# The recurrent core of an RWKV-7 block: one mask for the whole triangle, and a new order of work on four engines

## The chip, the cores and the metric
One core of a Trainium2 chip runs the kernel. The metric is the time on the device, in microseconds (us), of one execution. TensorE multiplies matrices, VectorE and ScalarE work element by element, GpSimd does small side jobs, and SyncE issues DMAs.

## What is computed
The reference runs two transformer blocks over 1024 tokens of width 1024. The part at hand is the third mixer of the first block, `rwkv7_time_mix`, with 6 heads of 64 columns:

```python
def step(state, inp):
    r_t, w_t, k_t, v_t, kk_t, a_t = inp
    sa = jnp.einsum('bhvk,bhk->bhv', state, kk_t)
    state = (state * w_t[:, :, None, :]
             - sa[..., :, None] * (kk_t * a_t)[..., None, :]
             + v_t[..., :, None] * k_t[..., None, :])
    return state, jnp.einsum('bhvk,bhk->bhv', state, r_t)
...
_, out = lax.scan(step, state0, tuple(seq_first))
```

A 64x64 state per head is scaled, corrected and added to at each of the 1024 tokens, and read out with `r`. Everything else of the two blocks (projections, the two other mixers, normalizations, two feed-forward networks, a second block with its own mixers) lies before and behind this part and is not changed.

## The kernel before
The kernel is written for each engine by itself. Every engine has its own program in a fixed order, and semaphores tie the programs together: `did(eng, ins, name)` (L280) raises a semaphore when an instruction ends and makes the engine wait for it, and `wait_ge` holds an engine for another one. There is no planner. An engine that waits holds everything written behind the wait.

The core (L429 to L692) replaces the scan by chunks of `CH` = 128 tokens, `NC` = 8 of them. Three **units** i = 0, 1, 2 hold two heads h each, and each half q of a chunk has 64 tokens, so that most products are 64x64. All are in float32, which is why the trace has two records for each product and only one for a transpose. Per chunk, in TensorE's order (`core_pe`, L585):
- **Transposes** (L594) of Z, B, KK and VV into `bank_a(i)`. ScalarE copies them to `seqmaj` (L509).
- **Score products** (L600): B and KK against Z and R, four products of 64x256 a unit, filling both PSUM banks of the unit. VectorE copies the 128x1024 result under a causal mask by `copy_predicated` with `keep` (`scores_copy`, L548).
- **Triangle products** (L611): Z against B within and across the halves. `first_inverse` (L552) puts them into the unit matrix that GpSimd has laid down (L500).
- **Values** (L620): scores times VV for the three units, into `PT[3]`; ScalarE copies them (L511).
- **Levels** (L625): five steps for blocks 2, 4, 8, 16, 32 invert the unit triangular matrix. In each, x = triangle times inverse (4 products a unit), then VectorE multiplies x by the level's mask from `const` (`x_masked`, L567), then t = inverse times masked x (8 products a unit, 4 in the last level), then VectorE adds t to the inverse (L572, L575).
- **Solves** (L645 to L663): three steps of 64x128 products with a copy by ScalarE after each (L515, L518, L521).
- **R and G** (L664), with an addition and a copy by VectorE (L578, L579); **outputs** o (L671) and **states** g (L676) of which most is multiplied before it is known how the chunk's state enters; then the two products with the scaled state (L682). ScalarE copies the output (L524), and VectorE makes the next state (L582). At the head of each chunk VectorE scales the state twice (L546, L547).

`bank_a(i)` and `bank_b(i)` are the two 512-column halves of the PSUM tensor `PT[i]`. SyncE's queue and the DMAs play no part in the core beyond loads for later stages, issued before it (L695). Ahead of the core stand the projections up to `o2` (L590 waits for it), behind it the group norm of the core's output (`after_core_pe`, L740).

## Time and profile before

| what | value |
|---|---|
| median of 3 runs | 2602.79 us (2601.04 to 2603.61) |
| profiled execution, span | 2601.7 us |
| the core in it | 370.7 to 601 us |
| TensorE, VectorE, ScalarE, GpSimd busy in the span | 94%, 56%, 34%, 35% |
| granted clock of TensorE, mean | 0.971 of full speed |

The profiled execution's own time is this span; it lies 1.1 us under the median of the runs and among them. In the rows further down times count from the start of the span. PE is TensorE, PEld its loads of weights, DVE VectorE, ACT ScalarE, POOL GpSimd. A form such as `64*128 64x256` is the shape of the weights' tile in the array (rows\*columns), then that of the moving operand. A view that merges records names the form of the first. The granted clock is given as a share of 2.4 GHz, and has two levels, 1.0 and 0.5 (1.2 GHz).

### The profile page before, as it was taken

The page shows a single profiled execution, that of the slowest core. Times are in us where ns is not written, and L with a number is a line of the kernel's source. Part 1 is how long each engine was busy: PE and PEld are TensorE (multiplying, and loading weights), DVE is VectorE, ACT ScalarE, POOL GpSimd, SP SyncE. Part 2 cuts the span into 40 slices and gives each one's busy share as a digit, 9 for nine tenths or more (in the row PEclk, how much of TensorE's full clock was granted, in tenths as well). Part 3 has the DMA queues.
Part 4 walks back from the last instruction along what each step waited for, and adds up shares of the span by engine and source line. Part 5 has one row for each costly group of instructions (what it writes and reads, how often), then busy time and mean ns, then how long its engine had stood idle before and what let it go on. Part 6 is the DMA issues. An engine that isn't in the chain of part 4 may idle for free.

```text
span 2601.7 us, 36870 instructions
## 1 busy us (share of the span) xinstructions
PE 2453.7 (94%) x14984; PEld 1447.0 (56%) x15146; DVE 1453.3 (56%) x1727; ACT 887.3 (34%) x1105; POOL 907.3 (35%) x502
## 2 busy tenths in 40 slices
PE   4989999999889999999998999999889999999997
PEld 1645558886445555555554566675345555555553
DVE  5975666663487640466405794355587640466414
ACT  3255422221145431354313323321155431255314
POOL 0312110000236532455324798101236531455331
PEclk7999999999999999999998999989999999999999
DMA  8611030000302122211313613300121122211322
GB/s 330 236 47 49 14 110 3 3 3 17 121 9 65 50 89 107 88 53 62 120 34 137 112 52 94 124 1 25 41 89 49 65 88 99 97 49 65 118 72 84
DMA packets 55369, 199.91 MB, mean 77 GB/s; under 512 B 5792, under 2 KB 15520, under 8 KB 52256
## 3 DMA queue, kind: packets, MB, share of 16 engines
q1 hardware_dynamic: 47424, 179.98, 20.5%
q10 hardware_dynamic: 7776, 17.56, 1.9%
q8 instruction: 120, 1.97, 0.3%
q14 instruction: 49, 0.40, 0.1%
HBM read 168.16 MB, written 29.36 MB: 76 GB/s over the span
## 4 chain that ended last, share of the span: by engine, by line
PE 77%; DVE 11%; POOL 4%; issue 3%; DMA 3%; ACT 2%; SPq 0%; ACTq 0%; DVEq 0%; POOLq 0%; another core or an unknown queue 0%
PE pt L1163 16%; PE pt L1169 15%; PE pt L1166 15%; PE pt L1748 10%; PE pt L587 7%; PE pt L425 3%; PE pt L728 2%; PE pt L2625 2%; PE pt L2631 2%; PE pt L2628 2%; DMA work<-in_w_mod 1%; DVE work L550 1%; PE pt L346 1%; PE pt L411 1%; DVE work L2883 1%
## 5 line engine op out<-in xcount | busy, mean ns | idle before, releaser
L1113 POOL TENSOR_TENSOR slots<-work,weights_rounded 128x512 bf16<-128x512 f32 (+2 forms) x239 | 435.1, 1820 | 607.4 <-ACT weights_rounded L1285 317.6
L1166 PE MATMUL pt<-work,weights_rounded 128*128 128x512 bf16 x1208 | 327.5, 385 | 2.2
L1163 PE MATMUL pt<-rounded,weights_rounded 128*128 128x512 f32 x624 | 210.4, 454 | 11.4 <-POOL slots L1113 5.9
L587 PE MATMUL pt<-work 64*64 64x64 f32 (+5 forms) x4512 | 212.0, 244 | 6.7 <-DVE work L550 5.5
L1163 PE MATMUL pt<-rhs_rounded,weights_rounded 128*128 128x512 f32 x624 | 210.6, 454 | 7.2 <-DVE work L845 4.2
L587 PEld LDWEIGHTS pt<-work 64*64 64x64 f32 (+3 forms) x4512 | 192.8, 142 | 26.0 <-DVE work L550 7.7
L1163 PE MATMUL pt<-hidden_rounded,weights_rounded 128*128 128x512 f32 x704 | 203.5, 424 | 0.3
L1166 PEld LDWEIGHTS pt<-work,weights_rounded 128*128 128x128 bf16 x1248 | 100.1, 99 | 169.1 <-issue 98.2
L1169 PE MATMUL pt<-hidden_rounded,slots 128*128 128x512 bf16 x691 | 176.6, 387 | 1.1
L1169 PE MATMUL pt<-rhs_rounded,slots 128*128 128x512 bf16 x607 | 168.9, 391 | 1.4 <-issue 0.2
L1169 PE MATMUL pt<-rounded,slots 128*128 128x512 bf16 x607 | 168.7, 390 | 1.4 <-issue 0.2
L1279 ACT ACTIVATE weights_rounded<-work 128x512 fp32r<-128x512 f32 x196 | 123.8, 632 | 132.5 <-PE pt L1169 127.3
L1166 PE MATMUL pt<-slots,weights_rounded 128*128 128x512 bf16 x674 | 166.9, 381 | 1.3
L1163 PEld LDWEIGHTS pt<-hidden_rounded,weights_rounded 128*128 128x128 f32 x704 | 131.8, 188 | 41.6 <-POOL slots L1113 2.4
L1113 POOL TENSOR_TENSOR slots<-slots,weights_rounded 128x512 bf16<-128x512 f32 (+1 forms) x86 | 128.8, 1497 | 65.2 <-ACT weights_rounded L1279 62.6
L1285 ACT ACTIVATE weights_rounded<-work 128x1408 fp32r<-128x1408 f32 x37 | 51.1, 1382 | 293.0 <-PE pt L1169 292.7
L1662 POOL TENSOR_TENSOR slots<-slots,weights_rounded 128x1024 bf16<-128x1024 f32 x28 | 66.7, 2382 | 238.6 <-ACT weights_rounded L2058 237.5
L1163 PEld LDWEIGHTS pt<-rounded,weights_rounded 128*128 128x128 f32 x624 | 118.5, 190 | 54.6 <-issue 8.2
L1163 PEld LDWEIGHTS pt<-rhs_rounded,weights_rounded 128*128 128x128 f32 x624 | 118.5, 190 | 50.3 <-issue 5.4
L2599 POOL TENSOR_TENSOR slots<-slots,weights_rounded 128x1024 bf16<-128x1024 f32 x21 | 56.6, 2696 | 238.5 <-ACT weights_rounded L2754 238.2
L1432 DVE TENSOR_TENSOR slots<-pt,slots 128x512 f32<-128x512 f32 x120 | 83.0, 691 | 86.7 <-PE pt L1169 84.1
L1166 PEld LDWEIGHTS pt<-slots,weights_rounded 128*128 128x128 bf16 x704 | 63.9, 98 | 92.5 <-issue 31.0
(393 smaller groups left out, 4089.8 us busy)
## 6 DMA issues: line engine op xcount, KB each, us to landing
work<-in_w_up SPq DMA_DIRECT2D x64, 512.0 KB, 4.0
work<-in_w_down SPq DMA_DIRECT2D x37, 704.0 KB, 4.1
work<-in_w_mod SPq DMA_DIRECT2D x10, 2048.0 KB, 8.5
slots<-in_w_in SPq DMA_DIRECT2D x31, 512.0 KB, 3.6
slots<-in_w_up SPq DMA_DIRECT2D x24, 512.0 KB, 4.8
x_scratch<-work ACTq DMA_DIRECT2D x16, 512.0 KB, 2.7
work<-x_scratch SPq DMA_DIRECT2D x16, 512.0 KB, 8.6
slots<-in_w_v SPq DMA_DIRECT2D x10, 512.0 KB, 4.1
```

What stands on the lines that cost most here:

```text
L425: ins = pe.matmul(pt(name)[:, h * 512:h * 512 + 512], weights(k), w(s)[:, h * 512:h * 512 + 512], start=(k == 0), stop=(k == n - 1))
L587: return pe.matmul(out, lhs, rhs, start=start, stop=stop, skip_group_check=True)
L728: ins = pe.matmul(pt(f"o{m}")[:, h * 512:h * 512 + 512], w(WRAW + (NJOBS1 + m) % 2)[:, k * P:(k + 1) * P], w(s)[:, h * 512:h * 512 + 512], ...
L1113: did(pool, pool.tensor_tensor(dst, raw, high.bitcast(F32), ALU.subtract), name)
L1163: pe.matmul(out, whi[:, k * P:k * P + P], rhs_hi(k), start=first and k == ks[0], stop=False, skip_group_check=True)
L1166: pe.matmul(out, top_half(whi)[:, k * P:k * P + P], rhs_lo(k), start=False, stop=False, skip_group_check=True)
L1169: ins = pe.matmul(out, wlo[:, k * P:k * P + P], top_half(rhs_hi(k)), start=False, stop=last and k == ks[-1], skip_group_check=True)
L1279: did(act, act.activation(flat_hi(fast_block(half, j, p), 512), block_raw(half, j, BLOCKS[p]), ACT.Copy), "ffn_w_hi")
L1432: did(dve, dve.tensor_tensor(dst, src0, src1, ALU.add), "ffn_post")
L1662: G_(pool.tensor_tensor(p1_lo(n), p2_raw(n), p1_hi(n).bitcast(F32), ALU.subtract), "w_split")
L1748: return pe.matmul(o, l, r, start=start, stop=stop, skip_group_check=True)
L2599: did(pool, pool.tensor_tensor(p1_lo(n), p1_raw(n), p1_hi(n).bitcast(F32), ALU.subtract), "w_split")
```

## The change
- **Masks.** The level masks in `const` are turned over, and VectorE multiplies the raw triangle by all five at once when it is there (`begin`, 128x640 from PSUM into `CD[i]`). x then comes out masked, and ScalarE copies it to SBUF instead of VectorE multiplying it (`x_kept`).
- **Inverse in two places.** Even chunks keep it in `CB_[i]`, odd ones in `CD[i]`. So the next chunk's triangle products and `begin` are written between this chunk's level 4 and its solves.
- **Scores between levels.** The products of a unit become KK against Z and R (64x256), B against R (64x128) and only one 64x64 corner of B against Z, each head in a bank of its own; they and their copies (two of 128x448 a unit) stand between the levels. The transposes stand between levels 0 and 1.
- **States in the next chunk.** Outputs and state products of chunk c - 1 (`ends`) stand inside level 0 of chunk c, in `bank_b`, unit by unit; the new state is made by VectorE after the adds of level 0. The last chunk's state isn't made. GpSimd scales the states.

TensorE's matrix work is otherwise the same. The diff, cut: the lines removed are those of the functions printed above, and of those added `solves` (the old code with the new names), some declarations and blank lines are left out.

```diff
-put(f"level{b}", (r64 // (2 * b) == k64 // (2 * b)) & ((r64 // b) % 2 == 1) & ((k64 // b) % 2 == 0))
+put(f"level{b}", (r64 // (2 * b) == k64 // (2 * b)) & ((r64 // b) % 2 == 0) & ((k64 // b) % 2 == 1))
...
+def crossing(i, h):
+    return w(CA[i])[half(0), h * 512 + 64:h * 512 + 128]
...
+def level_t(i, h, n, rows):
+    at = 128 + h * 320 + n * 64
+    return w(CD[i])[rows, at:at + 64]
...
+def score_bank(i, h):
+    return (bank_b(0), bank_b(1), bank_b(2), bank(7), bank_b(0), bank_b(1))[2 * i + h]
...
+def inverse(c, i):
+    return w(CD[i])[:, 768:1024] if c % 2 else w(CB_[i])[:, 0:256]
...
+    def units(c):
+        for i in range(3):
+            if c > 1:
+                pool.wait_ge(E("solve_done"), 9 * (c - 2) + 6 + i + 1)
+            did(pool, pool.tensor_copy(inverse(c, i).rearrange("p (x n) -> p x n", x=4),
+                                       const("unit").unsqueeze(1).to_broadcast([P, 4, 64])), "inverse_unit")
+    units(0)
+    pool.wait_ge(E("p_end"), 3)
+    for c in range(NC):
+        if c < NC - 1:
+            units(c + 1)
+        for i in range(3):
+            if c > 0:
+                pool.wait_ge(E("state_new"), 3 * (c - 1) + i + 1)
+            did(pool, pool.tensor_scalar(s_scaled(i), state(i), small(PMID + 8 * i + c), None, ALU.mult), "pool_step")
+            did(pool, pool.tensor_scalar(s_ended(i), s_scaled(i), small(PEND + 8 * i + c), None, ALU.mult),
+                "state_scaled")
+def core_act(act):
+    act.wait_ge(E("core_zeroed"), 6)
+    def x_kept(c, n, i):
+        act.wait_ge(E("x_done"), 15 * c + 3 * n + i + 1)
+        did(act, act.activation(xbuf(i), x_of(i), ACT.Copy), "x_kept")
+    def o_kept(c):
+        for i in range(3):
+            act.wait_ge(E("o_done"), 3 * c + i + 1)
+            did(act, act.activation(w(Z + i)[:, c * CH:(c + 1) * CH], bank_b(i)[:, 256:384], ACT.Copy), "o_kept")
     for c in range(NC):
         for i in range(3):
+            x_kept(c, 0, i)
+        if c > 0:
+            o_kept(c - 1)
         for i in range(3):
             act.wait_ge(E("transposed"), 3 * c + i + 1)
-            did(act, act.activation(w(CC[i])[:, 0:512], bank_a(i), ACT.Copy), "seq_major")
+            did(act, act.activation(w(CC[i])[:, 0:512], bank_b(i), ACT.Copy), "seq_major")
+            x_kept(c, 1, i)
+        for n in range(2, 5):
+            for i in range(3):
+                x_kept(c, n, i)
...
+    o_kept(NC - 1)
...
+    def begin(c, i):
+        dve.wait_ge(E("inverse_unit"), 3 * c + i + 1)
+        dve.wait_ge(E("l_done"), c + 1)
+        V_(dve.copy_predicated(heads(inverse(c, i)), keep[:, 512:640].unsqueeze(1).to_broadcast([P, 2, P]), l_of(i)),
+           "inverse_ready")
+        V_(dve.tensor_tensor(w(CD[i])[:, P:768].rearrange("p (h b n) -> p h b n", h=2, b=5),
+                             l_of(i)[:, :, 64:P].unsqueeze(2).to_broadcast([P, 2, 5, 64]),
+                             level_masks(), ALU.mult), "levels_ready")
+    def add(c, n):
+        for i in range(3):
+            dve.wait_ge(E("t_done"), 15 * c + 3 * n + i + 1)
+            if n < 4:
+                V_(dve.tensor_tensor(inverse(c, i), inverse(c, i), t_of(i), ALU.add), "inverse_ready")
+            else:
+                turned = heads(inverse(c, i))[:, :, 64:P]
+                V_(dve.tensor_tensor(turned, turned, heads(t_of(i))[:, :, 64:P], ALU.add), "inverse_ready")
+    def scores_copy(c, i):
+        dve.wait_ge(E("products_done"), 3 * c + i + 1)
+        for h in range(2):
+            V_(dve.copy_predicated(w(CA[i])[:, h * 512 + 64:h * 512 + 512], keep[:, 64:512],
+                                   score_bank(i, h)[:, 64:512]), "scores_kept")
+    def state_next(c):
+        for i in range(3):
+            dve.wait_ge(E("o_kept"), 3 * c + i + 1)
+            dve.wait_ge(E("state_scaled"), 3 * c + i + 1)
+            V_(dve.scalar_tensor_tensor(state(i), bank_b(i)[:, 192:256], small(PEND + 8 * i + c), s_ended(i),
+                                        ALU.mult, ALU.add), "state_new")
+    for i in range(3):
...
+        add(c, 0)
+        if c > 0:
+            state_next(c - 1)
+        add(c, 1)
+        scores_copy(c, 0)
+        add(c, 2)
+        scores_copy(c, 1)
+        add(c, 3)
+        scores_copy(c, 2)
+        add(c, 4)
+        if c < NC - 1:
             for i in range(3):
+                begin(c + 1, i)
...
+    def l_products(c):
+        if c > 0:
+            pe.wait_ge(E("mv_kept"), c)
+        for i in range(3):
+            for x, (left, right) in enumerate(((Z + i, B + i), (B + i, Z + i))):
+                for h, q in ((0, 0), (1, 1), (0, 1), (1, 0)):
+                    at = h * 512 + i * P + x * 64
+                    ins = mm(PT[3][half(q), at:at + 64], w(left)[half(h), tok(c, q)], w(right)[half(h), tok(c, q)])
+        ins.then_inc(E("l_done"), 1)
+    def level_x(c, n):
+        for i in range(3):
+            pe.wait_ge(E("inverse_ready"), 18 * c + 3 * n + i + 1)
+            if n == 0:
+                pe.wait_ge(E("levels_ready"), 3 * c + i + 1)
+            for h in range(2):
+                for q in range(2):
+                    ins = mm(x_of(i)[half(q), h * 64:h * 64 + 64], level_t(i, h, n, half(q)),
+                             inv(c, i, h, 0, half(q)))
+            ins.then_inc(E("x_done"), 1)
+    def level_t_step(c, n):
+        for i in range(3):
+            pe.wait_ge(E("x_kept"), 15 * c + 3 * n + i + 1)
+            for h in range(2):
+                for q in range(2):
+                    if n < 4:
+                        mm(t_of(i)[half(q), h * P:h * P + 64], inv(c, i, h, 1, half(q)),
+                           xbuf(i)[half(q), h * 64:h * 64 + 64])
+                for q in range(2):
+                    ins = mm(t_of(i)[half(q), h * P + 64:h * P + P], xbuf(i)[half(q), h * 64:h * 64 + 64],
+                             inv(c, i, h, 1, half(q)))
+            ins.then_inc(E("t_done"), 1)
+    def transposes(c):
         for i in range(3):
             if c > 0:
                 pe.wait_ge(E("o_kept"), 3 * (c - 1) + i + 1)
+                pe.wait_ge(E("state_new"), 3 * (c - 1) + i + 1)
             for x, s in enumerate((Z + i, B + i, KK + i, VV + i)):
-                ins = pe.transpose(bank_a(i)[:, x * P:x * P + P], w(s)[:, tt], const("ident"))
+                ins = pe.transpose(bank_b(i)[:, x * P:x * P + P], w(s)[:, span_of(c)], const("ident"))
             ins.then_inc(E("transposed"), 1)
+    def products(c, i):
+        tt = span_of(c)
+        pe.wait_ge(E("seq_major"), 3 * c + (2, 3, 3)[i])
+        if i == 2:
+            pe.wait_ge(E("scores_kept"), 6 * c + 2)
+        for h in range(2):
+            mm(score_bank(i, h)[:, 256:512], w(KK + i)[half(h), tt], both(Z, i, 21, tt)[half(h)])
+        for h in range(2):
+            mm(score_bank(i, h)[:, 128:256], w(B + i)[half(h), tt], w(RR + i)[half(h), tt])
+        for h in range(2):
+            ins = mm(score_bank(i, h)[half(0), 64:128], w(B + i)[half(h), tok(c, 0)], w(Z + i)[half(h), tok(c, 1)])
+        ins.then_inc(E("products_done"), 1)
+    def values(c):
         for i in range(3):
+            pe.wait_ge(E("scores_kept"), 6 * c + 2 * i + 2)
...
+    def ends(c):
         for i in range(3):
             pe.wait_ge(E("r_ready"), 3 * c + i + 1)
+            pe.wait_ge(E("g_ready"), 3 * c + i + 1)
             pe.wait_ge(E("state_scaled"), 3 * c + i + 1)
             for h in range(2):
-                ins = mm(bank_a(i)[half(h), 256:384], s_scaled(i)[half(h)], rbuf(i)[half(h)], False, True)
+                mm(bank_b(i)[half(h), 256:384], zu(i)[:, h * P + 64:h * P + P], scores(i, h, 1), True, False)
+            for h in range(2):
+                mm(bank_b(i)[half(h), 256:384], seqmaj(i, 3, h), scores(i, h, 3), False, False)
+            for h in range(2):
+                ins = mm(bank_b(i)[half(h), 256:384], s_scaled(i)[half(h)], rbuf(i)[half(h)], False, True)
+            if c < NC - 1:
+                for h in range(2):
+                    mm(bank_b(i)[half(h), 192:256], seqmaj(i, 2, h), seqmaj(i, 3, h), False, False)
+                for h in range(2):
+                    mm(bank_b(i)[half(h), 192:256], seqmaj(i, 1, h), zu(i)[:, h * P + 64:h * P + P], False, False)
+                for h in range(2):
+                    ins = mm(bank_b(i)[half(h), 192:256], gbuf(i)[half(h)], s_scaled(i)[half(h)], False, True)
             ins.then_inc(E("o_done"), 1)
-            for h in range(2):
-                ins = mm(bank_b(i)[half(h), 192:256], gbuf(i)[half(h)], s_scaled(i)[half(h)], False, True)
-            ins.then_inc(E("chunk_done"), 1)
+    l_products(0)
+    for c in range(NC):
+        level_x(c, 0)
+        if c > 0:
+            ends(c - 1)
+        level_t_step(c, 0)
+        transposes(c)
+        level_x(c, 1)
+        level_t_step(c, 1)
+        products(c, 0)
+        level_x(c, 2)
+        products(c, 1)
+        level_t_step(c, 2)
+        level_x(c, 3)
+        products(c, 2)
+        level_t_step(c, 3)
+        level_x(c, 4)
+        values(c)
+        level_t_step(c, 4)
+        if c < NC - 1:
+            l_products(c + 1)
+        solves(c)
+    ends(NC - 1)
```

## Rows read from the trace of the kernel before

**Rows 1.** Page, busy time and share; the core's stretch by engine (busy PE, PEld, DVE, ACT, POOL; clock; DMA).
```profile
PE 2453.7 (94%) x14984; PEld 1447.0 (56%) x15146; DVE 1453.3 (56%) x1727; ACT 887.3 (34%) x1105; POOL 907.3 (35%) x502
...
370.70:601.00 230.30, 223.15 (x4608) 203.18 (x4608) 155.51 (x408) 52.22 (x128) 8.40 (x21) 0.98 0.04 13
```

**Rows 2.** Timeline, TensorE: first transpose of chunks 0, 3, 4, 5; first product behind the core.
```profile
370.73 1.53 PE L598 MATMUL pt<-cst,work 128*128 128x128 f32 x12 [1.43 <-DVE work L737]
...
456.84 0.33 PE L598 MATMUL pt<-cst,work 128*128 128x128 f32 x1
...
484.98 0.33 PE L598 MATMUL pt<-cst,work 128*128 128x128 f32 x1
...
514.59 0.33 PE L598 MATMUL pt<-cst,work 128*128 128x128 f32 x1
...
601.05 2.38 PE L411 MATMUL pt<-work,cst 128*128 128x512 f32 x5 [0.50 <-ACT work L524]
```

**Rows 3.** Chain of waits, chunk 7: from level 0 to level 1.
```profile
579.56 3.69 PE pt L587 x92
583.27 2.51 PE pt L587 x72
```

**Rows 4.** Timeline, chunk 7: start, length, engine, line, count, idle before.
```profile
575.05 2.64 DVE L550 COPY_PREDICATED work<-keep,pt 128x1024 f32<-128x1024 int32 x2 [0.50 <-PE pt L587]
577.75 1.59 PE L587 MATMUL pt<-work 64*64 64x64 f32 x24 [0.46 <-DVE work L550]
...
579.56 20.99 PE L587 MATMUL pt<-work 128*128 128x64 f32 x484 [0.22 <-DVE work L550]
...
583.25 0.94 DVE L567 TENSOR_TENSOR work<-pt,cst 128x128 f32<-128x128 f32 x3
583.26 2.38 PEld L587 LDWEIGHTS pt<-work 64*64 64x64 f32 x72 [0.16 <-DVE work L572]
584.39 1.35 DVE L572 TENSOR_TENSOR work<-work,pt 128x256 f32<-128x256 f32 x3 [0.20 <-PE pt L587]
```

**Rows 5.** Views of single lines: length in ns as min/median/max.
```profile
L509 ACT ACTIVATE work<-pt x24: 597/597/599, 371.5 to 574.4; 128x512 f32<-128x512 f32 x24
...
L524 ACT ACTIVATE work<-pt x24: 277/277/277, 398.6 to 600.5; 128x128 f32<-128x128 f32 x24
...
L500 POOL COPY work<-cst x24: 400/400/614, 339.6 to 568.3; 128x256 f32<-128x256 f32 x24
...
L550 DVE COPY_PREDICATED work<-keep,pt x24: 1294/1302/1304, 373.4 to 578.2; 128x1024 f32<-128x1024 int32 x24
...
L555 DVE COPY_PREDICATED work<-keep,pt x24: 441/444/449, 376.1 to 580.0; 128x256 f32<-128x256 int32 x24
```

**Rows 6.** Timeline cut at single records: last of a shape, first of the next.
```profile
570.68 0.40 PE L587 MATMUL pt<-work 128*64 128x64 f32 x8
...
571.04 0.48 PE L587 MATMUL pt<-work 128*64 128x64 f32 x3
...
571.19 0.33 PE L587 MATMUL pt<-work 64*64 64x128 f32 x2
...
570.19 0.22 DVE L579 COPY work<-pt 128x64 f32<-128x64 f32 x1
...
573.60 0.27 PE L598 MATMUL pt<-cst,work 128*128 128x128 f32 x1
573.80 0.49 PE L587 MATMUL pt<-work 64*128 64x256 f32 x2
```

**Rows 7.** Stretches of the core: busy time by engine, then granted clock.
```profile
370.10:373.50 3.40, 2.77 (x24) 2.49 (x26) 2.16 (x8) 1.79 (x3) 0.00 (x0) 1.00 0.91 283
...
404.20:407.60 3.40, 2.73 (x42) 2.34 (x44) 3.01 (x6) 0.41 (x1) 0.00 (x0) 1.00 0.00 0
407.60:411.00 3.40, 3.40 (x71) 3.40 (x69) 1.70 (x5) 0.08 (x1) 0.00 (x0) 0.51 0.02 5
...
434.90:438.30 3.40, 3.18 (x66) 2.92 (x66) 2.81 (x7) 0.49 (x1) 0.00 (x0) 1.00 0.02 7
```

More of the change, by code:

```diff
@@ L496, in core_pool @@
             for c in range(NC):
                 for i in range(3):
-                    if c > 0:
-                        pool.wait_ge(E("solve_done"), 9 * (c - 1) + 6 + i + 1)
-                    did(pool, pool.tensor_copy(inverse(i).rearrange("p (x n) -> p x n", x=4),
-                                               const("unit").unsqueeze(1).to_broadcast([P, 4, 64])), "inverse_unit")
-        def core_act(act):
-            act.wait_ge(E("core_zeroed"), 6)
-            for c in range(NC):
-                tt = slice(c * CH, (c + 1) * CH)
+                    x_kept(c, 0, i)
@@ L576, in core_dve @@
                 for i in range(3):
                     dve.wait_ge(E("rg_done"), 3 * c + i + 1)
-                    V_(dve.tensor_tensor(rbuf(i), bank_b(i)[:, 0:P], w(RR + i)[:, tt], ALU.add), "r_ready")
+                    V_(dve.tensor_tensor(rbuf(i), bank_b(i)[:, 0:P], w(RR + i)[:, c * CH:(c + 1) * CH], ALU.add), "r_ready")
                     V_(dve.tensor_copy(gbuf(i), bank_b(i)[:, P:192]), "g_ready")
-                for i in range(3):
-                    dve.wait_ge(E("chunk_done"), 3 * c + i + 1)
-                    V_(dve.scalar_tensor_tensor(state(i), bank_b(i)[:, 192:256], small(PEND + 8 * i + c), s_ended(i),
-                                                ALU.mult, ALU.add), "state_new")
@@ L644, in core_pe, with solves @@
+            def solves(c):
                 pe.wait_ge(E("mv_kept"), c + 1)
@@ L691, in core_pe @@
+            ends(NC - 1)
             pe.wait_ge(E("o_kept"), 3 * NC)
-            pe.wait_ge(E("state_new"), 3 * NC)
         def after_core_sp(sp):
```

128 lines of the change are left out of this document (23 added, 105 removed).

## The prediction, made before the changed kernel ran

> **What bounds the kernel now.** I read the page first: TensorE is busy for 94% of 2601.7 us [rows 1], and its records inside the recurrent core fill 223.15 of 230.30 us, VectorE's only 155.51 and ScalarE's 52.22 [rows 1]. All lengths below are us. The reader should not take 223 of 230 for a full engine: a record lasts 0.22 to 0.27 while the next pair of records begins 0.06 (64 columns wide) or 0.11 (128 wide) later, so waits shorter than a record's tail don't show.
>
> Next the starts of the chunks [rows 2]. The chunk from 456.84 to 484.98 takes 28.14, the one from 484.98 to 514.59 takes 29.61; the core takes 601.05 - 370.73 = 230.3. The slower chunks hold a fall of the granted clock [rows 7]. The profile has three in the core, 3.4 long each (half speed for 10.2 of 230.3 makes the mean of 0.98 [rows 1]), at 1.3 to 1.5 a chunk, 4.3 together; without them the core is 226.0.
>
> Then the chain of waits and the timeline of one chunk [rows 3, 4]. A level of the triangle's inverse takes 2.53 (583.27 to the next mask at about 585.80). In it VectorE does three masks (0.94) and three adds (1.35) with 0.20 idle, so TensorE waits for VectorE three times a level. The level's 36 products come in steps of 0.058, that is 2.10. In the stage of the scores TensorE stands for 0.46 and 0.22 behind the predicated copies of 1.30 [rows 4, 5].
>
> I make a ledger of TensorE's in-order queue for one chunk. A step is 0.11 for 128 columns and 0.058 for 64 [rows 6]. Transposes 12 x 0.11 = 1.3; score products 12 x 0.217 = 2.6 (256 columns, twice 128); triangle products 12 x 0.058 = 0.7; values 12 x 0.112 = 1.3; levels 4 x 2.1 + 1.4 = 9.8; solves 36 x 0.109 = 3.9; R and G 3 x 0.34 = 1.0; outputs and states 3 x 1.0. Sum 23.7 (unrounded). The rest of 28.14 is 4.4: changes of the tile's shape, and waits.
>
> **The price of a change of shape.** This is the term that the forecast hangs on. The last product of shape `128*64` starts at 571.04 and the first of shape `64*64` at 571.19, 0.15 later, though pairs of one shape come every 0.06 (eight records in 0.40, one lasting 0.22) [rows 6]. No wait explains it: the copy that this product needs ended at 570.41 [rows 6]. From transposes to the score products it is 573.60 to 573.80, 0.20 where 0.11 is usual [rows 6]. So a change costs 0.09 to 0.10. The first record of the new shape lasts 0.32, not 0.27, and its successor follows 0.05 late. I take 0.145. Before, a chunk has 8 changes, 1.2 in all; that leaves 3.3 for waits: 4 x (2.53 - 2.10) = 1.7 in the levels, 0.5 at their two ends, and 1.1 among scores, triangle and values (0.46 and 0.22 of it in view [rows 4]).
>
> The Trainium skill ("TensorEngine Tiling (Array Packing)", Key Properties) says that changing the tiling mode drains TensorE. If that meant a drain to the last record's end, a change would cost about 0.22, by the record's length in the row, and the sum below would rise by some 17 x 8 x 0.075 = 10; the row's 0.145 decides, and this stays out of the sum.
>
> **What the change removes.** The masks leave the levels, and the score copies and triangle wait leave the chunk's head: the 3.3 of waits go. The score products lose the B x Z quarter of each unit down to one 64x64 corner: 0.87 to 0.77, three times, -0.3.
>
> **What it adds, in TensorE's order** (unit = one of three head pairs).
>
> 1. Shapes. Outputs and states of the chunk before now stand in `ends`, unit by unit: `128*64`, `64*64`, `128*64`, `64*64`, four changes a unit, 12. Each `products` goes `64*64` to `64*128` and back, 6. Transposes inside the levels 2, values 2, and rows elsewhere 3. That is 25 against 8: 17 x 0.145 = +2.5 a chunk. Bounds: 0.05 a change (they may hide in waits) gives 0.9, 0.22 gives 3.7.
> 2. State. `transposes` now waits for `state_new`, which VectorE makes only after the three adds of level 0. After the last product: 0.28 to the add's start (tail and semaphore, as the 0.20 idle before the adds [rows 4]), 0.42 add, 0.32 state update (a 128x64 two-input operation, between the 128x64 copy of 0.22 [rows 6] and a 0.42 add), 0.05 back: 1.07 idle. Queued behind are level 1 and everything else.
> 3. ScalarE. It takes turns: a copy of 512 columns (0.60), then a copy of level 1's product (0.28) [rows 5]. With 0.035 between operations that is 0.94 a unit against 0.52 of TensorE's level step, so TensorE waits 0.13, 0.43 and 0.43, and restarts 0.05 late each time: 1.1.
> 4. The last adds of levels 2 and 3 trail TensorE: 0.33 each, 0.7. Values wait 0.1 for the last score copy: two copies of 128x448, each about 0.66 by interpolation between 0.44 and 1.30 [rows 5].
> 5. Costed at nothing: the multiplication by five masks, 128x640, about 0.81 (0.42 for 256 columns plus 1.016 ns for each further one), three times beside 4.9 of solves and R. VectorE has 3.98 for `begin` there and 0.9 to spare; at 1.3 each it would still be hidden in a steady chunk, and its cover gone it costs its whole excess. GpSimd's two state products a unit: no row has them; the nearest is its copy of 256 columns at 0.40 [rows 5]; six at up to 1.0 end some 15 before `ends` needs them. VectorE's sum is about 17 in 29.9, so it is not the bound. The next triangle's products wait for the copy of the values (0.5 on ScalarE) beside level 4's last products and trail by under 0.1. No DMA is moved.
>
> Waits now: 1.07 + 1.1 + 0.7 + 0.1 = 3.0 less what coincides with a change of shape (0.1). Period: 23.7 - 0.3 + 25 x 0.145 (3.6) + 2.9 = 29.9, against 28.14: **+1.8 a chunk**. What was taken away in waits comes back as waits, and the changes of shape are on top.
>
> Head and tail: the first level waits for three units of `begin`: 0.98 for the triangle products, 3 x 1.32, then 0.3: 5.25 to the first level step. The first period lacks the state wait, 28.9. Six more at 29.9. From the last start to the end 27.2 (no triangle, level 0 or state products behind it). Sum 5.25 + 28.9 + 179.5 + 27.2 = 240.9, plus 0.2 as between the last copy and 601.05 [rows 2]: 241.1 against 226.0, **+15.1**.
>
> **The clock.** The stretch before a fall had TensorE busy 2.73 of 3.40, and the clock in the next was 0.51 of 2.4 GHz, that is 1.2 GHz; a stretch with 3.18 kept 1.00 [rows 7]. In the new order the stretch around the 1.07 idle holds about 2.5 of 3.4, once a chunk, and level 1's waits follow. So I expect falls in six chunks rather than three. At 1.4 each that is +4.1. Nothing to twelve is possible. Total +19.2.
>
> **Rivals.**
>
> *Shapes are free (faster).* If changes cost only where TensorE would otherwise run through, and the extra 17 cost nothing, 8 x 17 x 0.145 = 19.7 comes off: 15.1 - 19.7 = -4.6, clock as before, 2598. It decides once a change costs under 0.145 - 15.1 / 136 = 0.034. For it: many changes stand next to waits. Against it: of the 17, all 12 in `ends` and 5 others stand where nothing is waited for, and the satisfied wait in rows 6 still paid. Chance 0.12.
>
> *About even.* Changes at 0.05, other waits as summed, or two of the waits of points 2 to 4 overlapping: 2604. Chance 0.08.
>
> *The clock falls in every chunk and again in level 1.* Idle 1.07, then level 1 with waits. Eight to twelve more falls than now at 1.4 is +11 to +17 instead of +4: 2631. Against it: the opening stretch with the transposes, busy only 2.77 of 3.40, kept its clock [rows 7]; half the cost would hide under ScalarE's copies. The Trainium skill ("TensorE: Matmul & The Clock Gate", Part 4: PE-mode transpose) says that transposes don't count as busy in the same way; by it idle and transposes would make one quiet stretch in every chunk and this rival would be the result. By that rule, the stretch at 370.10 should have been followed by a fall, and it was not. Chance 0.15.
>
> *The change doesn't do what it says:* masks leave the loop but VectorE is no freer. By the sum it drops from 19.4 to 17 a chunk; too little to hold TensorE. Within the forecast.
>
> **How the numbers follow.** Forecast 0.65: 2601.7 + 19.2 = 2620.9 by the profiled execution, whose span is 1.1 under the median of 2602.8; I say 2621, with 2611 to 2632 as its own range (a change at 0.11 to 0.18 is -5 to +5, falls -4 to +7, not both at their ends). Low end 2605: changes at 0.07 and no more falls than now, 15.1 - 136 x 0.075 = +4.9, and up to 1.6 of overlap among waits. High end 2636: the clock's rival with dearer changes. A measurement of this kernel can tell 0.2%, 5.2 us, from no change. Faster 0.12, the first rival; same 0.08, the second; slower 0.80.
>
> **What would show it.** Right: chunks near 29.9 where the clock holds; about 25 changes of shape a chunk, each 0.09 over its step; TensorE idle about 1.1 before the transposes, ended by L582's successor, and 0.4 before two of level 1's steps, ended by ScalarE; more falls than three. Wrong: chunks under 28.1; steps without the extra 0.09 inside `ends`; or waits for VectorE's five-mask product or GpSimd, which I cost at nothing.

## The result, and the profile after

The change makes the kernel slower: a median of 2621.59 us (2617.99 to 2624.64) against 2602.73 for the kernel before, run beside it on the same chip; the ratio is 1.0077, with an interval of 1.0063 to 1.0091. The profiled execution's own time is 2619.35, its span 2617.5. One execution of run 12 below took 2832.49, at a mean granted clock of 0.83 where all others have 0.96 or more, and is left out of its median and ratio. All lengths below are us.

The core is measured from its first instruction on TensorE to the first product of L411 behind it: 371.77 to 615.83, that is 244.06, where before it was 230.32 [rows 2]. The rest of the span is 2373.4, and was 2371.4. So 13.7 of the 15.8 between the two profiled spans lie in the core. Three lines of the page of the changed kernel (busy time by engine; then the two groups of L644: busy and mean ns, then idle before and what ended most of it):

```profile
PE 2472.9 (94%) x15206; PEld 1442.1 (55%) x15206; DVE 1427.9 (55%) x1604; ACT 920.5 (35%) x1225; POOL 930.3 (36%) x550
...
L644 PE MATMUL pt<-work 64*64 64x64 f32 (+2 forms) x4572 | 216.2, 241 | 9.4 <-ACT work L543 4.3
...
L644 PEld LDWEIGHTS pt<-work 64*64 64x64 f32 (+1 forms) x4572 | 188.1, 138 | 38.3 <-issue 11.8
```

The core's stretch of the changed kernel by engine, columns as in [rows 1]:

```profile
371.80:615.80 244.00, 228.62 (x4668) 199.40 (x4668) 127.56 (x285) 85.49 (x248) 25.76 (x60) 0.99 0.04 12
```

The edit does what its text says: VectorE falls from 155.51 to 127.56, ScalarE rises from 52.22 to 85.49 and GpSimd from 8.40 to 25.76. TensorE has 15.4 without a record, of which 9.4 stand before the products of L644, and nearly half of those behind ScalarE's copies.

Timeline of TensorE in the changed kernel: the first product of the core, the first transposes of chunks 4, 5 and 6 (now between levels 0 and 1), and the first product behind the core.

```profile
371.77 0.93 PE L644 MATMUL pt<-work 64*64 64x64 f32 x48 [1.43 <-DVE work L833]
...
501.17 0.30 PE L692 MATMUL pt<-cst,work 128*128 128x128 f32 x1 [1.01 <-DVE work L618]
...
531.08 0.30 PE L692 MATMUL pt<-cst,work 128*128 128x128 f32 x1 [1.00 <-DVE work L618]
...
561.00 0.30 PE L692 MATMUL pt<-cst,work 128*128 128x128 f32 x1 [1.00 <-DVE work L618]
...
615.83 0.70 PE L411 MATMUL pt<-work,cst 128*128 128x512 f32 x1 [0.44 <-ACT work L548]
```

A chunk takes 29.91 (531.08 to 561.00; five of the seven periods agree within 0.01), as forecast. The first two are 30.99 and 30.19; the first begins at 380.16, before the fall of the clock in the core's head has ended (run 8). The timeline of a steady chunk, all engines, has the two waits that the sum held:

```profile
529.26 1.35 DVE L603 TENSOR_TENSOR work<-work,pt 128x256 f32<-128x256 f32 x3 [5.06 <-PE pt L644]
530.65 0.93 DVE L618 SCALAR_TENSOR_TENSOR work<-pt,small,work 128x64 f32<-128x64 f32 x3
...
531.08 1.50 PE L692 MATMUL pt<-cst,work 128*128 128x128 f32 x12 [1.00 <-DVE work L618]
...
533.07 0.28 ACT L543 ACTIVATE work<-pt 128x128 f32<-128x128 f32 x1 [0.67 <-PE pt L644]
...
533.37 0.60 ACT L557 ACTIVATE work<-pt 128x512 f32<-128x512 f32 x1
...
534.00 0.28 ACT L543 ACTIVATE work<-pt 128x128 f32<-128x128 f32 x1
...
534.33 0.68 PE L644 MATMUL pt<-work 64*64 64x64 f32 x16 [0.26 <-ACT work L543]
...
534.94 0.28 ACT L543 ACTIVATE work<-pt 128x128 f32<-128x128 f32 x1
...
535.27 10.97 PE L644 MATMUL pt<-work 64*64 64x64 f32 x230 [0.25 <-ACT work L543]
```

TensorE is idle for 1.00 until VectorE's first state update (0.28, begun at 530.65) ends. Further on, ScalarE takes turns: a copy of 0.60 ahead of each of the next two copies of 0.28 (those at 534.00 and 534.94). TensorE is idle for 0.26 and 0.25 behind them; with the tail of the last record, about 0.17 (0.22 long, 0.058 to a next step), that is 0.43 each.

The price of a change of shape, in the middle of `ends`, at single records of the changed kernel:

```profile
526.53 0.29 PE L644 MATMUL pt<-work 128*64 128x64 f32 x4
526.59 0.43 PE L644 MATMUL pt<-work 128*64 128x64 f32 x4
526.75 0.27 PE L644 MATMUL pt<-work 64*64 64x64 f32 x2
```

Two pairs of one shape begin at 526.53 and 526.59, 0.06 apart; the first pair of the new shape begins at 526.75, 0.16 after the last of the old, and the pair behind it at 526.85, 0.106 later where 0.058 is usual. Nothing is waited for there: `ends` waits for R, G and the scaled state ahead of the unit's first product. The product at 526.75 adds to a result that was written just before, so one could ask whether that costs the time. The way back to `128*64` answers it: each unit's first product in `ends` begins a new result, and in all 18 such places between 425 and 600 it starts 0.147 to 0.149 behind the record before it, where 0.052 is usual. The trace has 184 changes in the core against 55 before, 17 more a chunk.

### The profile page after: what moved, and what is told of

It reads as the page before. It is cut to its first block, busy times and chain, and to the rows that moved or that the text cites. A ratio compares the mean times of both kernels' runs of the same rounds, so it can differ in the third digit from the quotient of the medians.

```text
span 2617.5 us, 37236 instructions
## 1 busy us (share of the span) xinstructions
PE 2472.9 (94%) x15206; PEld 1442.1 (55%) x15206; DVE 1427.9 (55%) x1604; ACT 920.5 (35%) x1225; POOL 930.3 (36%) x550
## 4 chain that ended last, share of the span: by engine, by line
PE 79%; DVE 10%; POOL 3%; issue 3%; ACT 3%; DMA 2%; ACTq 0%; DVEq 0%; POOLq 0%; SPq 0%
PE pt L1259 16%; PE pt L1265 15%; PE pt L1262 15%; PE pt L1844 11%; PE pt L644 7%; PE pt L425 3%; PE pt L824 2%; PE pt L2721 2%; PE pt L2727 2%; PE pt L2724 2%; DMA work<-in_w_mod 1%; PE pt L346 1%; PE pt L411 1%; DVE work L1489 1%; DVE work L2979 1%
## 5 line engine op out<-in xcount | busy, mean ns | idle before, releaser
L1262 PE MATMUL pt<-work,weights_rounded 128*128 128x512 bf16 x1248 | 334.0, 385 | 0.0
L644 PE MATMUL pt<-work 64*64 64x64 f32 (+2 forms) x4572 | 216.2, 241 | 9.4 <-ACT work L543 4.3
L644 PEld LDWEIGHTS pt<-work 64*64 64x64 f32 (+1 forms) x4572 | 188.1, 138 | 38.3 <-issue 11.8
L1262 PE MATMUL pt<-slots,weights_rounded 128*128 128x512 bf16 x704 | 172.6, 381 | 0.0
```

The lines of the kernel that those rows point to most:

```text
L644: return pe.matmul(out, lhs, rhs, start=start, stop=stop, skip_group_check=True)
L1262: pe.matmul(out, top_half(whi)[:, k * P:k * P + P], rhs_lo(k), start=False, stop=False, skip_group_check=True)
```

## The experiments

Two theories stood at first. **A** is the prediction's ledger: TensorE's queue is all that counts, a change of shape costs about 0.145 wherever it stands, and the waits of points 2 and 3 add to it. **B** is the first rival in a sharper form: a change of shape costs next to nothing by itself, and the time is in the two waits. The period of a steady chunk is the finest measure of them, since it mostly repeats within 0.02. Where a fence has two first products of transposes, they are the timeline's of that kernel in chunks 4 and 5.

**1. The ends grouped by shape.** TensorE does the products of `ends` that need the scaled state behind those of all three units, which takes ten changes out of a chunk.

```diff
                         mm(bank_b(i)[half(h), 256:384], seqmaj(i, 3, h), scores(i, h, 3), False, False)
-                    for h in range(2):
-                        ins = mm(bank_b(i)[half(h), 256:384], s_scaled(i)[half(h)], rbuf(i)[half(h)], False, True)
                     if c < NC - 1:
...
+                for i in range(3):
+                    for h in range(2):
+                        ins = mm(bank_b(i)[half(h), 256:384], s_scaled(i)[half(h)], rbuf(i)[half(h)], False, True)
+                    if c < NC - 1:
```

> The changed kernel with the products of `ends` in another order: first the 128*64 products of outputs and states for all three units, then all 64*64 products with the scaled state. Same products, same waits at the same place; 10 changes of the tile's shape fewer a chunk. Theory A (every change of shape costs about 0.145 us, wherever it stands): 10 x 0.145 = 1.45 a chunk, so chunks of 28.46 instead of 29.91, and the kernel 10 us faster than the changed one, near 2611. Rival B (the changes are free or hide in waits, and the loss is all waits for VectorE and ScalarE): chunks stay near 29.9 and the time near 2621.

Timeline of this kernel, chunks 4 and 5:

```profile
494.75 0.30 PE L692 MATMUL pt<-cst,work 128*128 128x128 f32 x1 [1.01 <-DVE work L618]
...
523.18 0.30 PE L692 MATMUL pt<-cst,work 128*128 128x128 f32 x1 [1.00 <-DVE work L618]
```

The period is 28.44: 1.47 less for ten changes, 0.147 each, and the state's wait is as long as ever. The core takes 233.46 and the ratio to before is 1.0030 (1.0017 to 1.0042). An order of TensorE's instructions alone is worth 10.6 of the core.

**2. Before, with its shapes mixed.** The opposite edit in the kernel before: `128*64` and `64*64` products of the outputs and states alternate by unit, six changes more a chunk, no other wait.

```diff
-                    for h in range(2):
-                        mm(bank_b(i)[half(h), 192:256], seqmaj(i, 2, h), seqmaj(i, 3, h), True, False)
-                    for h in range(2):
-                        mm(bank_b(i)[half(h), 192:256], seqmaj(i, 1, h), zu(i)[:, h * P + 64:h * P + P], False, False)
-                for i in range(3):
                     pe.wait_ge(E("r_ready"), 3 * c + i + 1)
...
                     for h in range(2):
+                        mm(bank_b(i)[half(h), 192:256], seqmaj(i, 2, h), seqmaj(i, 3, h), True, False)
+                    for h in range(2):
+                        mm(bank_b(i)[half(h), 192:256], seqmaj(i, 1, h), zu(i)[:, h * P + 64:h * P + P], False, False)
+                    for h in range(2):
                         ins = mm(bank_b(i)[half(h), 192:256], gbuf(i)[half(h)], s_scaled(i)[half(h)], False, True)
```

> The kernel before with one edit: the state products g (128*64) stand between the two 64*64 products of each unit in the chunk's last stage, instead of ahead of them. No product, wait or copy is added; 6 changes of shape more a chunk. Theory A: 6 x 0.145 = 0.87 a chunk, chunks of 29.0 instead of 28.14, the kernel 7 us slower than before, near 2610. Rival B: no difference, 2603.

```profile
488.06 0.33 PE L598 MATMUL pt<-cst,work 128*128 128x128 f32 x1
...
517.19 0.33 PE L598 MATMUL pt<-cst,work 128*128 128x128 f32 x1
```

These two starts are 29.13 apart; five of the seven periods are 29.03 against 28.14: 0.89 for six changes, 0.148 each. (The one at 29.13 answers to a 28.24 in the kernel before, run 9.) The ratio is 1.0028 (1.0013 to 1.0043). Added in one kernel and taken away in another, a change has the same price: theory B has nothing left to stand on, and the row of 0.145 was right.

**3. The state before the adds.** VectorE makes the new state before the adds of level 0.

```diff
-                add(c, 0)
                 if c > 0:
                     state_next(c - 1)
+                add(c, 0)
```

> The changed kernel with VectorE making the new states before the adds of level 0 instead of behind them. The wait of the transposes goes, nothing else moves. Ledger: 29.91 - 1.07 + about 0.1 that stays at the adds = 28.94 a chunk, the kernel 7 us faster than the changed one, near 2615. If the idle at the transposes is covered by something else that is late (ScalarE's copy of the output), chunks stay above 29.5.

Timeline of this kernel in chunk 5:

```profile
524.97 0.28 DVE L618 SCALAR_TENSOR_TENSOR work<-pt,small,work 128x64 f32<-128x64 f32 x1 [1.31 <-ACT work L548]
525.28 1.33 DVE L603 TENSOR_TENSOR work<-work,pt 128x256 f32<-128x256 f32 x3
...
525.82 1.53 PE L692 MATMUL pt<-cst,work 128*128 128x128 f32 x12
```

The transposes now follow the products with no idle time, while VectorE is still at its adds. The period is 28.87: -1.04, where point 2 had 1.07. The ratio is 1.0069 (1.0049 to 1.0090).

**4. ScalarE's turns.** Two transposed units are copied ahead of level 1's products and the third behind them.

```diff
+                def seq_kept(i):
                     act.wait_ge(E("transposed"), 3 * c + i + 1)
                     did(act, act.activation(w(CC[i])[:, 0:512], bank_b(i), ACT.Copy), "seq_major")
...
+                seq_kept(0)
+                seq_kept(1)
+                for i in range(3):
                     x_kept(c, 1, i)
+                seq_kept(2)
```

> The changed kernel with ScalarE copying the transposes of units 0 and 1 first, then the three products of level 1, then the transposes of unit 2, instead of taking turns. Ledger: level 1's three waits of 0.13, 0.43 and 0.43 with restarts go, 28.97 a chunk, the kernel 7.5 us faster than the changed one, near 2614. If level 1 waits for something else (the adds, or VectorE), less than 3 us.

Timeline of this kernel in chunk 5:

```profile
527.05 1.50 PE L697 MATMUL pt<-cst,work 128*128 128x128 f32 x12 [1.00 <-DVE work L623]
...
528.48 5.71 PE L649 MATMUL pt<-work 64*64 64x64 f32 x131
...
529.04 0.90 ACT L543 ACTIVATE work<-pt 128x128 f32<-128x128 f32 x3
```

TensorE runs through level 1 for 5.71 without a wait. The period is 28.97: -0.94, where point 3 had 1.1. The ratio is 1.0074 (1.0051 to 1.0097).

**5. Both waits mended, shapes left as they are.** The edits of 3 and 4 together. This is where A and B differ most: B holds that the new waits were the whole loss, and would have 26.5.

> The changed kernel with the two waits mended and the shapes left as the change has them: 24 changes of shape a chunk. Theory A: 29.91 - 0.97 - 0.94 = 28.0 a chunk, no better than the 28.14 of before, kernel 2600 to 2605: the removed waits only pay for the added changes of shape. Rival B (shapes free, only waits matter): the waits gone, chunks near 26.5.

```profile
491.72 0.33 PE L697 MATMUL pt<-cst,work 128*128 128x128 f32 x1
...
519.65 0.33 PE L697 MATMUL pt<-cst,work 128*128 128x128 f32 x1
```

27.93: A's number. The two waits are worth 1.98 together, the sum of what they were worth alone (1.04 and 0.94). With them gone the new order is ahead of the old by 0.21 a chunk, though the core still takes 228.63 against 226.13 (run 9), for its head has the bare `begin` and a fall of the clock (run 8). The ratio is 1.0028 (1.0014 to 1.0041).

**6. All three.** Edits 1, 3 and 4 together.

> The changed kernel with the three edits together: `ends` grouped by shape, new states ahead of level 0's adds, ScalarE's copies of the transposes of units 0 and 1 ahead of level 1's copies. If the three costs are separate terms of TensorE's queue (theory A), they add: 29.91 - 1.45 - 0.97 - 0.94 = 26.55 a chunk, the core some 218 us, the kernel near 2591, 0.4 to 0.5% faster than before. If they hide each other (one wait takes the place of another), chunks stay above 27.5 and the kernel at 2598 or more.

```profile
485.94 0.33 PE L697 MATMUL pt<-cst,work 128*128 128x128 f32 x1
...
512.39 0.33 PE L697 MATMUL pt<-cst,work 128*128 128x128 f32 x1
```

26.45: the three are worth 3.46 a chunk, and 1.47 + 1.04 + 0.94 = 3.45. Three terms of the sum are thus shown to be separate and to add. The core takes 218.19, that is 12.1 less than before's first profile and 25.9 less than the change's. Yet the ratio is 0.9993 (0.9983 to 1.0003): nothing that can be told from no change. Where the rest went is taken up under runs 9 to 12.

**7. The copies of x on VectorE.** In the change's own order, VectorE copies x instead of ScalarE.

```diff
                 for i in range(3):
+                    dve.wait_ge(E("x_done"), 15 * c + 3 * n + i + 1)
+                    V_(dve.tensor_copy(xbuf(i), x_of(i)), "x_kept")
+                for i in range(3):
                     dve.wait_ge(E("t_done"), 15 * c + 3 * n + i + 1)
```

> The changed kernel with one part undone: VectorE, not ScalarE, copies the (already masked) x of each level to SBUF, ahead of the level's adds. If giving the copies to ScalarE is what relieves the levels, this costs 1 or more a chunk. By the ledger it doesn't: VectorE has the time (15 more copies of 0.29 a chunk), and level 1 no longer queues behind ScalarE's 0.60 copies: 29.7 a chunk, 0 to 2 us faster than the changed kernel.

The periods are 29.61 against 29.91. Two among them are 29.90 and 29.93; in both, ScalarE's copy of the values (L553) starts 0.3 later than in the others, and the trace doesn't show why. The ratio is 1.0072 (1.0053 to 1.0091). So "copies by ScalarE" brings nothing in the order that the change gives it. By the ledger, what it saves in the other levels it loses in level 1, where ScalarE has the transposed units to copy as well. With ScalarE's turns mended the period is 28.97 (run 4), 0.64 under that of this run.

**8. The head filled.** All three, and chunk 0's transposes and their copies stand ahead of level 0, where TensorE waits for `begin`.

```diff
             l_products(0)
+            transposes(0)
             for c in range(NC):
...
-                transposes(c)
+                if c > 0:
+                    transposes(c)
```

> As all_three, and chunk 0's transposes and their copies stand ahead of its level 0, where TensorE is idle while VectorE lays out the first triangle. 12 transposes and two changes of shape, 1.6, move into that idle: the core 1.6 shorter than in all_three, steady chunks the same 26.55. If the fall of the clock in the head (375.5 in the changed kernel) comes from that idle, it goes too, another 1 to 2. Kernel 2588 to 2590.

The reason for this run is the one low stretch of the clock in the changed kernel's core. Stretches of the changed kernel's head and of a steady chunk, columns as in [rows 7]:

```profile
371.77:375.50 3.73, 1.38 (x56) 1.13 (x56) 2.53 (x4) 0.28 (x1) 0.00 (x0) 1.00 0.96 319
375.50:378.90 3.40, 2.62 (x44) 2.49 (x46) 1.54 (x3) 0.55 (x2) 0.00 (x0) 0.50 0.94 342
378.90:382.30 3.40, 3.40 (x36) 3.28 (x33) 0.99 (x3) 0.60 (x1) 0.00 (x0) 0.50 0.01 3
...
528.50:531.90 3.40, 2.40 (x60) 2.29 (x59) 2.12 (x6) 0.37 (x2) 0.70 (x2) 1.00 0.01 2
531.90:535.30 3.40, 2.89 (x65) 2.34 (x63) 0.59 (x2) 2.53 (x6) 1.95 (x5) 1.00 0.00 0
```

In the changed kernel TensorE is busy for 1.38 of 3.73 while it waits for `begin`, then its clock is 0.50 of 2.4 GHz (1.2 GHz) for 6.8. All nine profiles of the new order with this bare head have that fall there, 6.8 long, whatever else was edited. In a steady chunk it is busy for 2.40 of 3.40 around the state's wait, and keeps 1.00. The same stretches of this run's head:

```profile
372.10:375.50 3.40, 2.82 (x68) 2.41 (x68) 2.22 (x4) 1.72 (x3) 0.00 (x0) 1.00 1.00 316
375.50:378.90 3.40, 2.05 (x63) 1.97 (x65) 2.12 (x5) 0.91 (x4) 0.00 (x0) 1.00 0.98 353
378.90:382.30 3.40, 3.38 (x89) 3.05 (x84) 2.00 (x5) 0.83 (x3) 0.00 (x0) 1.00 0.06 19
```

With transposes in the gap the clock stays at 1.00, in the one profile that there is of this kernel. The core takes 214.69, 3.5 less than in run 6: 1.6 is the expectation's estimate for the work moved into the gap, and 1.9 is left for the clock. The median is 2593.23 (twelve executions, 2591.79 to 2595.92) and the ratio 0.9972 (0.9961 to 0.9984): this version beats both kernels, before by some 7 and the change by some 27 (by the two ratios, 0.9972 and 1.0077, since the two ran on different chips).

**9 to 12. The same kernels once more.** The core's gain in run 6 doesn't show in the total. Nor does all of it in other runs: the periods of runs 3 to 6 came out within 0.1 of what was expected, but their totals, and run 8's, were higher by 3 to 9 (2618.97 for 2615, 2618.23 for 2614, 2608.04 for 2600 to 2605, 2600.13 for 2591, 2593.23 for 2588 to 2590). The totals of runs 1 and 2, 2609.36 and 2607.92, were not. **Theory C** says that the rest of the program varies from one execution to the next by several us, with the clock, and that one profile of each is too few. **Theory D** says that a shorter core in the new order makes the rest longer. Before is run twice more, the change and run 6 once more, without any edit.

> The kernel before, unchanged, profiled again, to see what of a run's time belongs to the core and what varies outside it. The core holds 226.0 without falls of the clock and up to 4.3 more with three. Theory C (the rest of the program varies by chance, by where the clock falls): what lies outside the core differs from the 2371.4 of the first profile by several us. Rival D (the rest is the same in every execution of one kernel, and longer with the new order of the core): within 1 us of 2371.4.

> As before_b, a third execution of the kernel before. Theory C: the three differ by several us outside the core. Rival D: within 1 us.

> The changed kernel, unchanged, profiled again. The core should be the same 29.91 a chunk and 242 to 246 in all. Outside the core the first profile has 2373.4. Theory C: several us off that, overlapping with those of the kernel before. Rival D: 2373 to 2374 again.

> all_three, unchanged, profiled again. Core 218 again, 26.45 a chunk. Its first profile had 2380.8 outside the core, 9 more than the kernel before, which ate what the core had gained. Theory C: that is chance in good part, and this one is lower. Rival D: 2380 to 2381 again, a cost that the shorter core brings.

The medians are 2600.11 and 2602.33 for before (0.9998, 0.9981 to 1.0014; 0.9999, 0.9986 to 1.0012), 2620.55 for the change (1.0089, 1.0064 to 1.0113) and 2595.88 for run 6 (0.9979, 0.9968 to 0.9991). The spans of all profiles are taken apart here. Low clock is the time at about 0.5 outside the core, added up from the clock's records in the trace (the last record of each ends about 2 behind the span). The last column is what the kernel's median has over before's on the same chip, less what its core has over 226.13: what the total lost outside the core. Each of these is uncertain by 3 to 6, by the intervals of the ratios, and takes before's core without falls, which one of its three profiles isn't.

| kernel | span | core | the rest | low clock in the rest | lost outside, by medians |
|---|---|---|---|---|---|
| before, run 9 | 2592.5 | 226.13 | 2366.4 | 134 | -1.7 |
| before, first | 2601.7 | 230.32 | 2371.4 | 141 | |
| before, run 10 | 2600.7 | 226.13 | 2374.6 | 148 | 0.6 |
| before, mixed | 2602.6 | 233.25 | 2369.3 | 145 | -1.3 |
| changed, run 11 | 2614.7 | 244.20 | 2370.5 | 135 | 0.7 |
| changed, first | 2617.5 | 244.06 | 2373.4 | 141 | 0.9 |
| grouped | 2609.2 | 233.46 | 2375.7 | 158 | -0.1 |
| VectorE copies | 2618.6 | 241.97 | 2376.6 | 146 | 4.2 |
| both waits | 2605.4 | 228.63 | 2376.8 | 148 | 5.5 |
| all three, run 12 | 2595.2 | 218.13 | 2377.1 | 148 | 2.1 |
| copies after | 2615.4 | 236.56 | 2378.8 | 152 | 5.7 |
| head | 2594.1 | 214.69 | 2379.4 | 148 | 4.6 |
| state first | 2616.7 | 236.80 | 2379.9 | 171 | 6.2 |
| all three, run 6 | 2599.0 | 218.19 | 2380.8 | 155 | 8.0 |

For C: one and the same kernel before has 2366.4 to 2374.6 outside the core, and in each set of profiles of one kernel the longer rest goes with the longer low clock. Against C alone: the kernels edited from the change have 2375.7 to 2380.8, above all that before shows, and by their medians all but grouped lose 2 to 8 outside the core.

The instructions behind the core are the same in all fourteen, so the traces can be laid side by side from the core's end on. They differ in three places. In the first 163, the change and grouped take as long as run 9, and both waits, all three, copies after and state first 4.3 to 4.8 longer, with the others between; but so does run 10 (4.7), which is before without an edit. That part is C's. In a later feed-forward stage of 230, before (mixed or not) takes 229.9 to 230.0 and the ten profiles of the new order 231.0 to 234.0. And from VectorE's 41st-last instruction to the end the four of before take 59.9 and the ten 61.0 to 62.9, with 13 to 17.5 of low clock there against 9.3 to 9.6. One part of the second place can be seen. Timelines of VectorE and GpSimd there, run 9 first, then run 12:

```profile
1907.20 4.95 DVE L1381 TENSOR_TENSOR work<-work 128x512 f32<-128x512 f32 x4
...
1908.88 2.73 POOL L1120 TENSOR_TENSOR weights_rounded<-work,cst 128x1024 fp32r<-128x1024 f32 x1 [26.67 <-issue]
...
1906.64 7.00 DVE L1484 TENSOR_TENSOR work<-work 128x512 f32<-128x512 f32 x4
...
1907.82 2.50 POOL L1223 TENSOR_TENSOR weights_rounded<-work,cst 128x1024 fp32r<-128x1024 f32 x1 [26.61 <-issue]
```

The same four operations of VectorE take 4.95 and 7.00: one of them takes 2.77 instead of 0.69 in run 9, the one that runs beside GpSimd's, and two do in run 12 (2.77 and 2.74), where GpSimd starts just before the third of the four instead of just behind its start. Two are caught in eight of the ten profiles of the new order, one in grouped, in state first and in all four of before. So D holds in part: the last two places together cost 2.7 to 6.2, between 2.7 and 4.0 in all but head, in every kernel of the new order. But the change has them as well (3.6 and 2.9), so they don't come with a shorter core. Why GpSimd starts earlier there, and why the clock falls once more at the end, stays open: no run holds the end of the core fixed and moves these.

These runs brought a second thing. Timeline and stretches of run 9, before without an edit:

```profile
484.82 0.33 PE L598 MATMUL pt<-cst,work 128*128 128x128 f32 x1
...
513.06 0.33 PE L598 MATMUL pt<-cst,work 128*128 128x128 f32 x1
```

```profile
404.20:407.60 3.40, 2.73 (x62) 1.98 (x58) 3.27 (x4) 0.00 (x0) 0.00 (x0) 1.00 0.00 0
407.60:411.00 3.40, 3.38 (x88) 3.23 (x90) 2.75 (x8) 0.49 (x1) 0.00 (x0) 1.00 0.02 5
```

This chunk takes 28.24, and five others 28.14 or 28.15. In this execution and in the next the clock never falls in the core, and the core takes 226.13 in both; it doesn't fall there in run 2's kernel either. TensorE was busy for 2.73 of 3.40, as in [rows 7] ahead of a fall, and the clock held. (Run 9's core starts 1.2 later; the stretch with the very same work, 405.40 to 408.80, has 2.74 and no fall behind it either.) The three falls and their 4.2 belong to one execution of the kernel before, not to its order of work.

## Why the prediction came out right, and where it was wrong

**The ledger.** It was right as a whole and in most of its terms. The core of before without falls was worked out at 226.0 from one disturbed profile; runs 9 and 10 have 226.13. The period of 29.9 came out at 29.91. The removed 3.3 of waits and 0.3 of score products were not tried one by one, but the mended order bears them out: it has 14 changes a chunk where before had 7, so by the ledger 28.14 - 3.3 - 0.3 + 1.0 and the 0.8 of point 4 make 26.3, and run 6 has 26.45. Single terms among these (the 3.3, the 0.3, the 0.8) may still be off against each other.

**The price of a shape.** Forecast 0.145, measured 0.147 and 0.148 in two opposite edits. The count was one too high on both sides: the traces have 7 and 24 a chunk, not 8 and 25, since I had counted a change at the solves that keeps its shape. The 17 more were right, and so were the 2.5. The Trainium skill ("TensorEngine Tiling (Array Packing)", Key Properties) says that a change of mode drains TensorE. The 0.10 by which the new shape starts late in the row is less than the 0.16 that a wait for the end of the last record would add; as the page of the profile models the ends of TensorE's records, this speaks against a full drain but doesn't rule it out.

**State and ScalarE.** The state's 1.07 measured 1.04. ScalarE's 1.1 measured 0.94: the two waits of 0.43 were there, and the term was 0.16 too large; it had 0.13 for a wait at the first unit, and the timeline of the steady chunk shows none there. They could be added up, with no overlap, as runs 5 and 6 show. Point 4 (adds of levels 2 and 3, 0.7) was not tried by itself.

**Costed at nothing.** The five-mask product takes 0.82 (forecast 0.81) and a pair of score copies 1.35 (forecast 2 x 0.66). GpSimd's two state products take 0.44 each beside the core's work, inside the bound of 1.0; ahead of the core, beside VectorE's operations of 128x1024 on `work` and `slots`, three take 1.53, 1.24 and 1.17. None of them makes TensorE wait in a steady chunk. The first level's wait for `begin` was forecast at 5.25; the timeline of the changed kernel has the third unit's products at 376.98, 5.21 behind the first instruction:

```profile
373.34 0.82 DVE L595 TENSOR_TENSOR work<-pt,cst 128x640 f32<-128x640 f32 x1
...
374.31 0.45 PE L644 MATMUL pt<-work 64*64 64x64 f32 x8 [1.61 <-DVE work L595]
...
376.98 3.25 PE L644 MATMUL pt<-work 64*64 64x64 f32 x56 [0.64 <-DVE work L595]
```

**The clock is the step that failed.** The prediction took a stretch with 2.73 of 3.40 busy as the mark of a fall, and expected falls in six chunks rather than three, +4.1. There is none in any steady chunk, in either profile of the change, though its quiet stretch is busy for only 2.40. The rule was drawn from one execution, and run 9 has the same 2.73 without a fall. The fall that did come is where the sum had looked for none, in the bare head, and takes about 2 (1.9 by run 8). The third rival, falls in every chunk, goes the same way: 1.00 idle with 1.50 of transposes behind it did not bring the clock down in seven chunks, and in run 8's head transposes stand in the gap and the clock stays up. The Trainium skill ("TensorE: Matmul & The Clock Gate", Part 4: PE-mode transpose) says that transposes don't count as busy in the same way. By that rule both places would have been quiet, and neither was followed by a fall.

**Why the number was right all the same.** This part was luck: two errors cancel. Against an execution of before without falls the change costs 244.1 - 226.1 = 18.0 in the core, where 15.1 was forecast: 2 of the rest is the head's fall and 1 lies at the two ends of the core and in its first two chunks, which were only estimated. The 4.1 for more falls was not there, but neither, in two of three profiles, were the 4.3 that before was thought to lose. Of the first pair of profiles 13.7 is in the core and 2.1 outside. The medians, 18.9 apart, lie by the forecast's 19.2, and nearer to the 18.0 than to the 13.7; of the forecast's mechanism they bear out the 15.1, not the 4.1.

**The rivals.** Shapes free, 2598: ruled out by runs 1 and 2. About even, 2604: it wanted changes at 0.05 or waits that overlap; neither was found. That the change doesn't do what it says: the masks left the loop, and VectorE went from 19.4 to 16 a chunk, which freed an engine that was no longer waited for.

## What to carry to other kernels

Where an engine's in-order queue is the bound, write its ledger: steps by tile shape, a price for each change of shape, and each wait with what releases it. Three terms found that way in this profile were mended one by one, and the gains added to within 0.01 of 3.46 a chunk. Read the total as well: up to 8 of what the core gained was lost in stages that nobody had edited. A new order of work that hides one wait is easily paid for in changes of the tile's shape, so group what is moved by shape as well as by unit. Draw no rule for the clock from one execution: profile the unchanged kernel two or three times first.

## What the runs showed of the hardware

- A change of the tile's shape on TensorE costs 0.147 to 0.148 in float32 (runs 1 and 2), with every operand long there: behind a pair of 64 columns, the first pair of the new shape starts 0.16 rather than 0.06 after the last of the old, and its successor 0.05 late.
- TensorE's clock fell after a stretch with 2.73 of 3.40 busy in one execution and held after one with 2.73, with 2.40 and with 2.05 in others. It fell in all nine profiles in which the head has 1.38 of 3.73 or about that. Between executions of one kernel, with not a line changed, the span differs by 9 (2592.5 and 2601.7); 4.2 of that are the core's three falls.
- The time outside the core rises with the low clock there over the fourteen profiles, from 2366.4 at 134 to 2380.8 at 155; it does so loosely, with 2379.9 at 171.
- A VectorE operation of two SBUF operands (128x512, float32) takes 2.77 instead of 0.69 beside one of GpSimd's (128x1024, 2.4 to 3.0 long), in all fourteen profiles. GpSimd's of 128x64 takes 1.17 to 1.53 instead of 0.44 beside VectorE's of 128x1024; beside one of those that reads PSUM (367.97, in the changed kernel) it takes 0.44.
